# Borders between stages in two halves of 256 tokens, a part of the lower terms of h on GpSimd

## The reference, cut to what matters

```python
h = rms_norm(x, norm_g) * (1 + scale) + shift
x = x + 0.5 * gate * swiglu(h, w_in, w_down)      # F0, F1, F2, F3
x = x + gate * mixer(h)                           # attention (QKV, WO), hgrn2 (HIN, HO)
...
p = rmsnorm(x, g) @ w_in                          # P2, then OUT and the last norm
```

## Time and profile before

| what | value |
|---|---|
| device time, median of 3 runs | 2433.12 us (2431.3 to 2435.06) |
| profiled execution, span of its trace | 2435.2 us |
| PE busy | 2385.0 us, 98% |
| DVE busy | 1273.8 us, 52% |
| ACT busy | 861.1 us, 35% |
| POOL busy | 203.1 us, 8% |
| mean granted clock of PE | 0.992 |

### The profile page before, as it was taken

The page is one execution under the profiler, slowest core; times in us unless marked ns, Lnnn a source line. Parts: engine busy times, 40 slices in busy tenths (PEclk is TensorE's granted clock), DMA queues, the critical chain, the costliest instruction groups (busy, mean ns, idle before and its releaser), DMA issues.

```text
span 2435.2 us, 30379 instructions
## 1 busy us (share of the span) xinstructions
PE 2385.0 (98%) x11030; PEld 1908.2 (78%) x11030; DVE 1273.8 (52%) x1951; ACT 861.1 (35%) x1320; POOL 203.1 (8%) x337
## 2 busy tenths in 40 slices
PE   7999999999899999999999999999999999999998
PEld 4888888677588888888888878888888888867666
DVE  5886334455568883343333345554533333459554
ACT  3222223566443222232232243434432222344353
POOL 1212000000001110000000013331000000021100
PEclk9999999999999999999999999999999999999999
DMA  7899432321149983323333321222233333242221
GB/s 267 272 288 290 118 95 66 102 61 52 48 126 290 294 251 109 94 76 93 102 95 107 92 78 54 60 56 75 78 104 95 100 112 95 65 96 55 64 58 52
DMA packets 420386, 285.27 MB, mean 117 GB/s; under 512 B 22691, under 2 KB 397789, under 8 KB 420305
## 3 DMA queue, kind: packets, MB, share of 16 engines
q1 hardware_dynamic: 397888, 207.64, 29.4%
q0 software_dynamic: 20896, 73.80, 9.2%
q10 hardware_dynamic: 1520, 2.77, 0.3%
HBM read 281.85 MB, written 6.72 MB: 118 GB/s over the span
## 4 chain that ended last, share of the span: by engine, by line
PE 91%; DVE 3%; ACT 2%; DMA 1%; issue 1%; SPq 1%; POOL 0%; ACTq 0%; DVEq 0%; POOLq 0%
PE bank L666 13%; PE bank L667 13%; PE bank L668 13%; PE bank L834 7%; PE bank L836 7%; PE bank L835 7%; PE bank L1442 4%; PE bank L1444 4%; PE bank L1443 4%; PE bank L1469 2%; PE bank L701 2%; PE bank L703 2%; PE bank L702 1%; PE bank L1087 1%; PE bank L1114 1%; PE bank L681 1%
## 5 line engine op out<-in xcount | busy, mean ns | idle before, releaser
L624 DVE TENSOR_TENSOR w_lo<-raw,w_hi 128x1024 fp32r<-128x1024 f32 (+1 forms) x333 | 435.7, 1309 | 430.3 <-ACT w_hi L606 425.7
L606 ACT ACTIVATE w_hi<-raw 128x1024 fp32r<-128x1024 f32 (+1 forms) x333 | 371.8, 1117 | 479.9 <-PE bank L668 243.0
L666 PE MATMUL bank<-h_hi,w_hi 128*128 128x512 f32 x1344 | 523.1, 389 | 1.8 <-DVE w_lo L624 1.8
L667 PE MATMUL bank<-h_lo,w_hi 128*128 128x512 f32 x1344 | 522.9, 389 | 0.0
L668 PE MATMUL bank<-h_hi,w_lo 128*128 128x512 f32 x1344 | 522.8, 389 | 0.0
L666 PEld LDWEIGHTS bank<-h_hi,w_hi 128*128 128x128 f32 x1344 | 252.3, 188 | 55.3 <-DVE w_lo L624 2.7
L668 PEld LDWEIGHTS bank<-h_hi,w_lo 128*128 128x128 f32 x1344 | 252.3, 188 | 52.4
L667 PEld LDWEIGHTS bank<-h_lo,w_hi 128*128 128x128 f32 x1344 | 252.3, 188 | 52.0
L834 PE MATMUL bank<-g_hi,w_hi 128*128 128x512 f32 x704 | 277.8, 395 | 0.0
L836 PE MATMUL bank<-g_hi,w_lo 128*128 128x512 f32 x704 | 276.0, 392 | 0.0
L835 PE MATMUL bank<-g_lo,w_hi 128*128 128x512 f32 x704 | 273.2, 388 | 0.0
(11 more groups left out here) (407 smaller groups left out, 3056.5 us busy)
## 6 DMA issues: line engine op xcount, KB each, us to landing
raw<-in_ffn_w_in SPq DMA_DIRECT2D x176, 512.0 KB, 3.9
ada<-in_ada_w POOLq DMA_DIRECT2D x128, 512.0 KB, 5.0
raw<-in_ffn_w_down SPq DMA_DIRECT2D x64, 704.0 KB, 4.6
raw<-in_hgrn_w_in SPq DMA_DIRECT2D x32, 512.0 KB, 4.1
raw<-in_attn_w_qkv SPq DMA_DIRECT2D x24, 512.0 KB, 3.8
raw<-in_w_in SPq DMA_DIRECT2D x22, 512.0 KB, 3.8
ada_first<-in_ada_w SPq DMA_DIRECT2D x16, 512.0 KB, 10.8
bias_scratch<-bias_lines POOLq DMA_DIRECT2D x14, 320.0 KB, 9.1
```

Of the source, the lines that this page charges most:

```text
L606: line(nc.scalar.activation(w_hi[:, n % 2, 0:k * P], raw[:, n % 4, 0:k * P], ACT.Copy), hi_ready)
L624: line(nc.vector.tensor_tensor(w_lo[:, n % 2, 0:k * P], raw[:, n % 4, 0:k * P], w_hi[:, n % 2, 0:k * P].bitcast(F32), ALU.subtract), lo_ready)
L666: nc.tensor.matmul(out_ap, wh, xh, start=(k == 0), stop=False)
L667: nc.tensor.matmul(out_ap, wh, xl, start=False, stop=False)
```

## The change

At each border the last tile of xT (the last two behind WO and HO) is multiplied for tokens 0 to 255 first (half 0), with a signal `half_out`, then for tokens 256 to 511 (half 1), in banks of their own; every matmul has 256 columns and each loads its weights again. `sums_pe` of half 0 stands inside the products of half 1, that of half 1 inside the next stage's products; the filler matmuls are gone. The next stage's first two blocks are multiplied as: block n with half 0, block n+1 with half 0, then both with half 1. ACT and DVE run through orders written out by hand (`border_act`, `border_dve`), in which blocks n-1, n and n+1 are split between the tiles. At borders 1 to 5 POOL makes h_lo of tiles 1, 3, 5, 7 of either half, by an addition of the shift in place in tmp and a subtraction. POOL does this for borders 1 and 2 before it issues the ada loads of F1. The first square of a stage is written to sumsq directly, so that no memset and no addition for tile 0 is left; the loops over the down tiles on DVE and ACT are written out. Border 0 (before F0) stays whole. TAKEN, ADDED and the functions of counts only work out semaphore values: `cols_of(half)` is the slice of 256 tokens; `halved(m)` is true for the borders behind WO and HO.

```diff
+POOLED = (1, 2, 3, 4, 5)
...
+def pair_tile(pe, m, half, k, b, banks):
+    c_ = cols_of(half) if m else slice(0, T)
+    n = FIRST[NEXT[m]] + b
+    wh, wl = w_hi[:, n % 2, k * P:(k + 1) * P], w_lo[:, n % 2, k * P:(k + 1) * P]
+    pe.wait_ge(hhi_ready, tile_count(m, half, k))
+    nc.tensor.matmul(banks[b][:, c_], wh, h_hi[:, k, c_], start=(k == 0), stop=False)
+    nc.tensor.matmul(banks[b][:, c_], wl, h_hi[:, k, c_], start=False, stop=False)
+    pe.wait_ge(hpool_ready if pooled(m, k) else h_ready, low_count(m, half, k))
+    return nc.tensor.matmul(banks[b][:, c_], wh, h_lo[:, k, c_], start=False, stop=(k == KD - 1))
...
+def product_pair(pe, m, banks):
+    n = FIRST[NEXT[m]]
+    if m == 0:
+        pe.wait_ge(lo_ready, n + 2)
+        pair_both(pe, m, 0, banks)
+        return
+    xb = x_base(BORDER[m]) + TAKEN.get(BORDER[m], 9)
+    pe.wait_ge(lo_ready, n + 1)
+    pe.wait_ge(x_ready, xb - 1)
+    for k in range(KD):
+        if k == 4:
+            sums_pe(pe, m, 1)
+        pair_tile(pe, m, 0, k, 0, banks)
+    pe.wait_ge(lo_ready, n + 2)
+    pe.wait_ge(x_ready, xb)
+    for k in range(KD):
+        pair_tile(pe, m, 0, k, 1, banks)
+    pair_both(pe, m, 1, banks)
...
-def idle_turns(count):
-    for _ in range(count):
-        nc.tensor.matmul(B[7][:, 0:P], ones[:, :], ones[:, :], start=True, stop=True)
-def norm_pe(pe, m):
-    pe.wait_ge(sum_ready, (KD - 1) * m)
-    nc.tensor.matmul(B[5][:, :], ones[:, :], sumsq[:, :], start=True, stop=False)
-    idle_turns(4)
-    pe.wait_ge(sq_ready, KD * (m + 1))
-    nc.tensor.matmul(B[5][:, :], ones[:, :], sq[:, :], start=False, stop=True).then_inc(rms_ps, 1)
-    idle_turns(14)
+def sums_pe(pe, m, half):
+    name, c_ = BORDER[m], cols_of(half)
+    sums = sum_base(name) + ADDED.get(name, 6)
+    squares = x_base(name) + TAKEN.get(name, 9)
+    pe.wait_ge(sum_ready, sums - 1 if halved(m) and half == 0 else sums)
+    nc.tensor.matmul(root_bank(half)[:, c_], ones[:, :], sumsq[:, c_], start=True, stop=False)
+    pe.wait_ge(sq_ready, squares if half else x_base(name) + KD)
+    nc.tensor.matmul(root_bank(half)[:, c_], ones[:, :], sq[:, c_], start=False, stop=True).then_inc(rms_ps, 1)
 def first_norm_pe(pe):
...
+def norm_tile_dve(dve, line, m, half, j):
+    c_ = cols_of(half) if m else slice(0, T)
+    if j >= 4:
+        dve.wait_ge(hpool_ready if pooled(m, j) else h_ready, low_count(m, half, j - 4))
+    line(nc.vector.scalar_tensor_tensor(out=tmp[:, j % 4, c_], in0=xT[:, j, c_], scalar=scale_col[:, j:j + 1],
+                                        in1=rstd[:, c_], op0=ALU.mult, op1=ALU.mult), t_ready)
...
+def norm_low_pool(pool, line, m):
+    for half in range(2):
+        c_ = cols_of(half)
+        for j in range(1, KD, 2):
+            t_ = tmp[:, j % 4, c_]
+            pool.wait_ge(hhi_ready, tile_count(m, half, j))
+            line(nc.gpsimd.tensor_scalar(t_, t_, mod[:, 24 * m + j:24 * m + j + 1], None, ALU.add))
+            line.settle()
+            line(nc.gpsimd.tensor_tensor(h_lo[:, j, c_], t_, h_hi[:, j, c_].bitcast(F32), ALU.subtract),
+                 hpool_ready)
...
+        norm_tile_dve(dve, line, m, half, j)
         if j:
-            lower(j - 1)
-    lower(KD - 1)
+            norm_low_dve(dve, line, m, half, j - 1)
+    norm_low_dve(dve, line, m, half, KD - 1)
+    if m in POOLED:
+        dve.wait_ge(hpool_ready, low_count(m, half, KD - 1))
     first_half_lo(dve, line, m)
...
+def border_act(act, line, m, after):
+    name = BORDER[m]
+    n, xb = FIRST[NEXT[m]], x_base(name)
+    split_hi(act, line, n - 1)
+    nc.scalar.preload_act_table_set("natural_log_exp_and_others")
+    if halved(m):
+        square_half_act(act, line, xb + 7, KD - 2, 0)
+        square_half_act(act, line, xb + 8, KD - 1, 0)
+        norm_root_act(act, line, m, 0)
+        norm_hi_act(act, line, m, 0, 0)
+        split_hi(act, line, n)
+        square_half_act(act, line, xb + 9, KD - 2, 1)
+        norm_hi_act(act, line, m, 0, 1)
+        norm_hi_act(act, line, m, 0, 2)
+        split_hi(act, line, n + 1)
+        square_half_act(act, line, xb + 10, KD - 1, 1)
+        norm_hi_act(act, line, m, 0, 3)
+    else:
+        square_half_act(act, line, xb + 8, KD - 1, 0)
+        norm_root_act(act, line, m, 0)
+        norm_hi_act(act, line, m, 0, 0)
+        norm_hi_act(act, line, m, 0, 1)
+        split_hi(act, line, n)
+        norm_hi_act(act, line, m, 0, 2)
+        norm_hi_act(act, line, m, 0, 3)
+        square_half_act(act, line, xb + 9, KD - 1, 1)
+        split_hi(act, line, n + 1)
+    norm_hi_act(act, line, m, 0, 4)
+    norm_root_act(act, line, m, 1)
+    for j in range(5, KD):
+        norm_hi_act(act, line, m, 0, j)
+    norm_rest_act(act, line, m, 1, after)
...
+def border_dve(dve, line, m):
+    name = BORDER[m]
+    n = FIRST[NEXT[m]]
+    outs = sum(2 if halved(q) else 1 for q in range(1, m))
+    split_lo(dve, line, n - 1)
+    norm_scale_dve(dve, line, m)
+    if halved(m):
+        dve.wait_ge(half_out, outs + 1)
+        residual_half_dve(dve, line, KD - 2, 0)
+        add_half_dve(dve, line, 0)
+        dve.wait_ge(half_out, outs + 2)
+        residual_half_dve(dve, line, KD - 1, 0)
+        dve.wait_ge(rstd_ready, root_count(m, 0))
+        norm_tile_dve(dve, line, m, 0, 0)
+        dve.wait_ge(used, n - 1)
+        residual_half_dve(dve, line, KD - 2, 1)
+        norm_tile_dve(dve, line, m, 0, 1)
+        norm_low_dve(dve, line, m, 0, 0)
+        split_lo(dve, line, n)
+        norm_tile_dve(dve, line, m, 0, 2)
+        norm_low_dve(dve, line, m, 0, 1)
+        add_half_dve(dve, line, 1)
+        dve.wait_ge(used, n)
+        residual_half_dve(dve, line, KD - 1, 1)
+        norm_tile_dve(dve, line, m, 0, 3)
+        norm_low_dve(dve, line, m, 0, 2)
+    else:
+        dve.wait_ge(half_out, outs + 1)
+        residual_half_dve(dve, line, KD - 1, 0)
+        dve.wait_ge(rstd_ready, root_count(m, 0))
+        norm_tile_dve(dve, line, m, 0, 0)
+        norm_tile_dve(dve, line, m, 0, 1)
+        norm_low_dve(dve, line, m, 0, 0)
+        split_lo(dve, line, n)
+        norm_tile_dve(dve, line, m, 0, 2)
+        norm_low_dve(dve, line, m, 0, 1)
+        norm_tile_dve(dve, line, m, 0, 3)
+        norm_low_dve(dve, line, m, 0, 2)
+        dve.wait_ge(used, n)
+        residual_half_dve(dve, line, KD - 1, 1)
+    norm_tile_dve(dve, line, m, 0, 4)
+    norm_low_dve(dve, line, m, 0, 3)
+    norm_tile_dve(dve, line, m, 0, 5)
+    norm_low_dve(dve, line, m, 0, 4)
+    split_lo(dve, line, n + 1)
+    norm_tile_dve(dve, line, m, 0, 6)
+    norm_low_dve(dve, line, m, 0, 5)
+    norm_tile_dve(dve, line, m, 0, 7)
+    norm_low_dve(dve, line, m, 0, 6)
+    norm_low_dve(dve, line, m, 0, 7)
+    norm_rest_dve(dve, line, m, 1)
+    norm_gate_dve(dve, line, m)
+RES_OF = {name: m for m, name in BORDER.items()}
...
+        pe.wait_ge(lo_ready, n + b + 1)
+        for k in range(KH):
+            last = down(None, 0, None, b, k, n + b)
+        last.then_inc(used, 1)
+    n = n0 + UP + 2 * (KD - 1)
+    pe.wait_ge(x_ready, xb + KD - 2)
+    for half in range(2):
+        for b in range(2):
+            pe.wait_ge(lo_ready, n + b + 1)
+            for k in range(KH):
+                if half == 1 and b == 0 and k == 5:
+                    sums_pe(pe, m, 0)
+                last = down(None, 1, half, b, k, n + b)
+            if half == 1:
                 last.then_inc(used, 1)
+            elif b == 1:
+                last.then_inc(half_out, 1)
...
+        product(pe, FIRST[name] + j, B[j % 2][:, :], xs, waits=(y_ready, ybase) if by_tile and j == 0 else None)
+    for half in range(2):
+        c_ = cols_of(half)
+        for j in (KD - 2, KD - 1):
+            n = FIRST[name] + j
+            pe.wait_ge(lo_ready, n + 1)
+            if half == 0:
+                pe.wait_ge(x_ready, xb + j - 1)
+            for k, (xh, xl) in enumerate(xs):
+                if half == 1 and j == KD - 2 and k == 4:
+                    sums_pe(pe, RES_OF[name], 0)
+                wh, wl = w_hi[:, n % 2, k * P:(k + 1) * P], w_lo[:, n % 2, k * P:(k + 1) * P]
+                bank = half_bank(j, half)[:, c_]
+                nc.tensor.matmul(bank, wh, xh[:, c_], start=(k == 0), stop=False)
+                nc.tensor.matmul(bank, wh, xl[:, c_], start=False, stop=False)
+                last = nc.tensor.matmul(bank, wl, xh[:, c_], start=False, stop=(k == KD - 1))
+            last.then_inc(used if half else half_out, 1)
 def back_act(act, line, name):
-    for j in range(KD):
-        if j or name not in ("WO", "OUT"):
+    for j in range(KD - 2):
...
             .then_inc(bias_out if h < HEADS else bias_out2, 16)
+    for m in (1, 2):
+        if m in POOLED:
+            norm_low_pool(pool, line, m)
     ada_loads(pool, 9, 9)
+    for m in (3, 4):
+        if m in POOLED:
+            norm_low_pool(pool, line, m)
     hgrn_pool(pool, line)
+    if 5 in POOLED:
+        norm_low_pool(pool, line, 5)
     pool.wait_ge(used, FIRST["P2"])
     second_pool(pool, line)
```

(73 more changed lines are left out.)

254 lines of the change are left out of this document (136 added, 118 removed).

## The result

| | before | after |
|---|---|---|
| median of 4 runs, us | 2432.21 (2430.98 to 2435.06) | 2472.91 (2470.94 to 2474.18) |
| ratio, 95% interval | | 1.0158 [1.0145, 1.0171] |
| profiled execution: own time, span | as shown ahead | 2474.18, 2472.6 |
| mean granted clock of PE in that execution | 0.992 | 0.983 |

The change makes the kernel 40.7 us slower. The forecast was +23, 2456; the sign and the range (2426 to 2479) held, the size did not. The granted clock was 0.983 to 0.986 in the four executions after the change.

The account below looks back on a forecast made before the run. PE, busy 98% of the span, bounds the kernel. Borders 1, 3, 4 add 9.9 us, borders 2 and 5 13.2, border 6 0.65, the start -0.5: together +23, 2456 us, range 2426 to 2479.

Parts of the forecast that it names:

- two parts, FFN border: Multiplying in two halves of 256 tokens, without GpSimd, makes a border behind an FFN stage 0.65 us longer.
- two parts, behind WO and HO: Multiplying in two halves, without GpSimd, makes each border behind WO and HO 2.2 us longer, 30.2 against 28.0.
- GpSimd, FFN border: POOL's slower lower parts and half the possible hold-up with DVE bring an FFN border's loss from 0.65 to 3.3 us.
- GpSimd, behind WO and HO: POOL's slower lower parts and half the possible hold-up bring the loss behind WO and HO from 2.2 to 6.6 us.
- clock, changed kernel: PE's granted clock at the borders: nothing in the forecast's sum, +10 us in all only as a rival, chance 0.10.
- start: Before the first tile of h, dropping the memset of sumsq saves 0.5 us.
- forecast's own case: Borders slower by the schedule, from +17 us without POOL and DVE holding each other up to +29; chance 0.45.
- B: At the borders the POOL and DVE lock covers the shift additions too: +44 us, 2477; chance 0.15.
- E: Half matmuls are dearer than 0.1175 us: each 0.01 us more gives +13 us, so 2468 and above; chance 0.05.
- C: New waits at the six borders lower PE's clock, 1.7 us lost each time: +10 us, 2466; chance 0.10.
- Rival D: Half 0's tiles come as PE needs them, its pair under 5 us: faster by 16 us, 2417, or 2425; chance 0.20.
- wait 1: PE waits at each border for block n-1's w_lo: 0.8 us at FFN borders, 1.2 behind WO and HO.

Follow-up runs that it names:

- run 2: Changed kernel with all lower parts on DVE, none on GpSimd, plus 12 filler matmuls a border in PE's waits of half 0: 2440.92 us, 1.0027.
- run 3: Changed kernel, GpSimd kept, with 19 filler matmuls at each border in PE's waits of half 0's pair: 2464.94 us, 1.012 to the kernel before.
- run 1: Changed kernel with no lower part on GpSimd, all on DVE, no fillers: 2445.72 us, 1.0036 to the kernel before.
- run 6: Changed kernel with GpSimd making the odd lower parts only in half 1, DVE those of half 0: 2446.89 us, 1.0044 to the kernel before.
- Run 4: Changed kernel without GpSimd's addition of the shift, so its output differs from the reference: 2449.57 us, 1.006 to the kernel before.
- run 5: Changed kernel with all lower parts on DVE; POOL issues the same kinds of operation on its own buffer, nobody waiting: 2451.26 us, 1.006.
- run 9: run 7 without fillers, ACT making h_hi 4 to 7 before half 1's rstd, DVE's tmp further ahead, block n+1's split later: 2430.27 us, 0.9984.
- run 7: run 2 with block n-1 split earlier, before the square and its addition of the tile before, on ACT and DVE: 2435.47 us, 1.0001.

## Why the prediction was right in sign and short in size

With runs 2 and 3 each term of the sum can be laid beside what it measured (us, per border where nothing else is said):

| term | forecast | measured |
|---|---|---|
| two parts, FFN border | 0.65 | 0.2 to 0.3 (run 2 less before) |
| two parts, behind WO and HO | 2.2 | 2.15 |
| GpSimd, FFN border | 2.65 (3.3 less 0.65) | 3.4 (run 3 less run 2) |
| GpSimd, behind WO and HO | 4.4 | 4.8 |
| clock, changed kernel | 0, or 10 in all as a rival | 13.4 in all (after less run 3, 12.0, and border 6) |
| start | -0.5 | not separable |

The measured terms add up to the borders' 38.5: 5.2 for the two parts, 19.9 for GpSimd and 13.4 for the clock. The last has 1.4 from border 6. There the changed kernel took 33.8, as run 1 did with the clock down, and run 6, with the clock at 1.00 and no fillers, took 32.3.

**The step that failed is the one that kept the clock out of the sum.** The prediction had the new waits, each below 3 us, had one stretch at a low clock behind a wait of 2.65 us, and gave this a chance of 0.10 as a case apart. It is no case apart: the low clock came together with the waits that the forecast itself had, in all four executions of the changed kernel (mean clock 0.983 to 0.986; the kernel before had 0.990 to 0.994 in 56 executions beside the experiments), and run 3, which fills these waits, has it back at 1.00. The largest single wait was 2.1 us, most were 0.7 to 1.4, and several followed each other; over half 0 of block n at border 1 PE was busy for half of the time (windows of the changed kernel):

```profile
408.18:417.60 9.42, 4.92 (x30) 3.89 (x29) 7.97 (x16) 6.23 (x13) 5.45 (x7) 0.94 0.38 111
```

The kernel before had fillers in its gap, the change took them out, and the forecast costed "the filler matmuls are gone" at nothing. The rival's 1.7 us for a fall came from a row of another stage and was a fair size: the borders lost 2.2 each on average (13.4 over six), and 1.3 in run 1.

**Second, GpSimd's term was short by 3.1 us** (19.9 against 16.75). The durations were the reason. The timeline of POOL at border 1:

```profile
409.14 0.93 POOL L903 TENSOR_SCALAR tmp<-tmp,mod 128x256 f32<-128x256 f32 x1 [1.32 <-ACT h_hi L846]
410.15 0.78 POOL L905 TENSOR_TENSOR h_lo<-tmp,h_hi 128x256 fp32r<-128x256 f32 x1
...
415.47 1.09 POOL L903 TENSOR_SCALAR tmp<-tmp,mod 128x256 f32<-128x256 f32 x1
416.64 0.72 POOL L905 TENSOR_TENSOR h_lo<-tmp,h_hi 128x256 fp32r<-128x256 f32 x1
```

The scalar operation took 0.93 to 1.09 here (forecast 0.8, upper bound 1.0), the subtraction 0.72 and more (0.61). Run 4 shows the lever: taking the first of the two away gives back 22.1 us, clock included. At the five borders the scalar operation had a mean of 1003 ns, the subtraction of 853.

That the result lies in the range is partly luck. The forecast's own case ended at +29, some 2462. The range reached as far as 2472.9 only for the sake of B and E, and neither was what happened; what filled the distance was the clock of C on top of a GpSimd term that was too small.

**Rival B was near in its number (2477) and wrong in its mechanism.** Its lock is visible in part. At border 1 of the changed kernel a POOL subtraction beside a DVE split took 1.69 us against the 0.78 of the next one. The timelines of DVE and of POOL:

```profile
405.99 1.23 DVE L683 TENSOR_TENSOR w_lo<-raw,w_hi 128x1024 fp32r<-128x1024 f32 x1 [0.87 <-ACT w_hi L665]
```

```profile
406.12 1.69 POOL L905 TENSOR_TENSOR h_lo<-tmp,h_hi 128x256 fp32r<-128x256 f32 x1
```

DVE's tmp operations went from 479 to 606 ns. But run 5, where POOL holds DVE up and nobody waits for POOL, costs some 5 us (5.2 by the medians, 5.5 at the borders), where 27 lie between B and the case without hold-up. Nor does POOL's scalar operation lock DVE out for its whole length: this lower part of DVE's (timeline, same kernel) began and ended within the 1.09 us of POOL's scalar operation of 415.47, 0.21 us longer than the 0.48 of one alone:

```profile
415.69 0.69 DVE L892 SCALAR_TENSOR_TENSOR h_lo<-tmp,mod,h_hi 128x256 fp32r<-128x256 f32 x1
```

The Trainium skill, page "SBUF — State Buffer", section on the two sides, has a VectorE operation with two SBUF inputs and a GpSimd operation that reads SBUF take one pair of ports in turn, and whichever comes second blocked for the whole of the other. The prediction wrote "any GpSimd operation"; all of POOL's operations here read SBUF, so that does not change the case. The subtraction behind the split roughly agrees (the split was done at 407.22, the subtraction 0.59 us later, where one takes 0.72). The row above does not, as far as POOL's rough spans can tell.

So the hold-up is real and the smaller part; what decides is the time until a tile's lower part is there. The part of it that falls on POOL itself (the 1.69) belongs to that time and was not separated.

**Rival D had its condition stated rightly.** The first 24 matmuls of the pair's half 0 took about 9 us at the FFN borders and 12.9 behind WO and HO, from the start of the first to that of the last, not under 5. In run 9 they took 4.7 and 5.9, and there the two parts pay: 178.8 against 184.9 at the borders. The forecast took the order written out as fixed, which for the change it was.

**What else held.** The half matmul (0.1175 forecast, 0.117 measured), rstd 12.3 us after the tile (tmp starts at 403.57, the tile had ended at 391.2), one wait on ACT's h_hi at an FFN border (1.06, forecast 1.4), POOL's h_lo as the largest group of waits (4.0 to 5.8 a border, forecast 3 to 5), the last tile of half 1 late (PE waits 0.65 there, forecast 0.7), wait 1 (0.55 and 0.9 shown, 0.8 and 1.15 given back in run 7). For the start, -0.5 was expected; but the changed kernel and run 1, alike up to there but for the order of POOL's ada loads, reach border 1's residual at 391.38 and 395.03, so one profile of each can't tell such a term.
